# Loading each expert weight block by two 1 MB transfers, each half with its own semaphore

## The reference, cut to what matters

```python
def swiglu(h, w_gate, w_up, w_down):
    return (jax.nn.silu(h @ w_gate) * (h @ w_up)) @ w_down

def moe_swiglu(h, w_router, w_gate, w_up, w_down):
    t = h.reshape(B * S, D)
    logits = (t @ w_router).astype(jnp.float32)
    top_vals, top_idx = lax.top_k(logits, TOP_K)
    top_w = jax.nn.softmax(top_vals, axis=-1)
    gates = jnp.sum(jax.nn.one_hot(top_idx, N_EXPERTS, dtype=jnp.float32) * top_w[..., None], axis=1)
    out = jnp.zeros_like(t)
    for e in range(N_EXPERTS):
        out = out + swiglu(t, w_gate[e], w_up[e], w_down[e]) * gates[:, e:e + 1]
```

## Time and profile before

| | |
|---|---|
| median of three runs | 1361.24 us |
| lowest, highest | 1359.88, 1361.25 us |
| the profiled execution's own time | 1359.71 us |
| its span, first to last instruction | 1357.9 us |
| instructions in it | 16939 |
| PE busy in the span | 97% |
| DVE, ACT busy | 58%, 49% |
| bytes moved by DMA | 451.63 MB, mean 333 GB/s |

### The profile page before, as it was taken

How to read it: one execution, slowest core, us unless ns; L and a number is a source line. 1 busy time by engine, 2 the same in 40 slices (tenths; PEclk the granted TensorE clock), 3 DMA queues, 4 the chain that set the end, 5 groups by cost and what they waited for, 6 DMA issues and landing times.

```text
span 1357.9 us, 16939 instructions
## 1 busy us (share of the span) xinstructions
PE 1322.0 (97%) x6365; PEld 942.0 (69%) x6365; DVE 790.1 (58%) x912; ACT 661.4 (49%) x823; POOL 41.2 (3%) x45
## 2 busy tenths in 40 slices
PE   9999999999999999999999999999998899999996
PEld 8888788888888877865666656666555566665562
DVE  6556355555569667965466564665445566544463
ACT  5444445444454764854455454554444455444451
POOL 1000001000000012000000000000000000000000
PEclk9999999999999999999999999999999999999999
DMA  9745446555455518999999999999999999999995
GB/s 381 308 154 184 166 174 238 191 191 187 148 192 186 219 64 330 428 428 428 406 426 428 426 428 427 412 426 428 426 429 426 413 427 427 428 428 429 425 428 214
DMA packets 40448, 451.63 MB, mean 333 GB/s; under 512 B 4873, under 2 KB 5001, under 8 KB 8368
## 3 DMA queue, kind: packets, MB, share of 16 engines
q1 hardware_dynamic: 37408, 440.82, 79.8%
q0 software_dynamic: 2816, 9.63, 1.8%
q10 hardware_dynamic: 144, 0.09, 0.0%
HBM read 445.52 MB, written 6.55 MB: 333 GB/s over the span
## 4 chain that ended last, share of the span: by engine, by line
PE 80%; DMA 16%; DVE 2%; ACT 1%; issue 0%; POOL 0%; SPq 0%; DVEq 0%; ACTq 0%
PE psum L2013 19%; PE psum L2015 19%; PE psum L2014 19%; PE psum L2401 15%; DMA raw<-in_moe_w_gu 5%; DMA raw_more<-in_moe_w_gu 4%; DMA raw_first<-in_moe_w_gu 2%; DMA work<-in_moe_w_gu 2%; DMA raw<-in_moe_w_down 2%; PE psum L2059 1%; PE psum L2061 1%; PE psum L2060 1%; PE psum L2069 1%; DVE w_lo L1427 1%; PE psum L2439 1%; PE psum L2432 1%
## 5 line engine op out<-in xcount | busy, mean ns | idle before, releaser
L1427 DVE TENSOR_TENSOR w_lo<-raw,w_hi 128x1024 fp32r<-128x1024 f32 (+1 forms) x148 | 262.7, 1785 | 206.8 <-ACT w_hi L1060 206.2
L1060 ACT CAST w_hi<-raw 128x1024 fp32r<-128x1024 f32 (+1 forms) x148 | 221.4, 1504 | 218.2 <-PE psum L2015 152.9
L2015 PE MATMUL psum<-w_hi,actA_lo 128*128 128x512 f32 (+1 forms) x752 | 290.8, 387 | 0.0
L2013 PE MATMUL psum<-w_hi,actA_hi 128*128 128x512 f32 (+1 forms) x644 | 256.6, 398 | 18.8 <-DVE w_lo L1427 17.6
L2014 PE MATMUL psum<-w_lo,actA_hi 128*128 128x512 f32 (+1 forms) x644 | 248.3, 386 | 0.0
L2013 PEld LDWEIGHTS psum<-w_hi,actA_hi 128*128 128x128 f32 x644 | 121.4, 189 | 63.5 <-DVE w_lo L1427 25.0
L2015 PEld LDWEIGHTS psum<-w_hi,actA_lo 128*128 128x128 f32 x752 | 141.7, 188 | 29.9
L2401 PE MATMUL psum<-raw_more,const 128*64 128x512 f32 x608 | 137.4, 595 | 0.0
L2014 PEld LDWEIGHTS psum<-w_lo,actA_hi 128*128 128x128 f32 x644 | 121.7, 189 | 22.0
L1427 DVE TENSOR_TENSOR w_lo<-raw_more,w_hi 128x1024 fp32r<-128x1024 f32 x54 | 65.0, 1223 | 93.7 <-ACT w_hi L1060 93.3
L2013 PE MATMUL psum<-w_hi,actB_hi 128*128 128x512 f32 x292 | 114.8, 393 | 0.0
(11 more groups left out here) (280 smaller groups left out, 1940.0 us busy)
## 6 DMA issues: line engine op xcount, KB each, us to landing
raw_more<-in_moe_w_gu SPq DMA_DIRECT2D x45, 2048.0 KB, 26.5
raw<-in_moe_w_gu SPq DMA_DIRECT2D x37, 2048.0 KB, 25.0
raw<-in_moe_w_down SPq DMA_DIRECT2D x20, 2048.0 KB, 25.5
raw_more<-in_moe_w_down SPq DMA_DIRECT2D x20, 2048.0 KB, 26.5
work<-in_moe_w_gu SPq DMA_DIRECT2D x16, 2048.0 KB, 21.4
raw_first<-in_moe_w_gu SPq DMA_DIRECT2D x14, 2048.0 KB, 25.4
raw<-in_ret_w_in SPq DMA_DIRECT2D x22, 1024.0 KB, 10.3
raw_first<-in_moe_w_down SPq DMA_DIRECT2D x8, 2048.0 KB, 26.2
```

The source lines that it names most:

```text
L1060: nc.scalar.copy(hi_of(u)[:, 0:size], raw_of(w, u)[:, 0:size]).then_inc(sem["hi_ready"], 1)
L1427: nc.vector.tensor_tensor(lo_of(u)[:, 0:size], raw_of(w, u)[:, 0:size], as_f32(hi_of(u)[:, 0:size]), ALU.subtract).then_inc(sem["lo_ready" ...
L2013: nc.tensor.matmul(dst, l_hi[:, k, cols], r_hi[:, kk, rcols], start=first, stop=False)
L2015: return nc.tensor.matmul(dst, l_lo[:, k, cols], r_hi[:, kk, rcols], start=False, stop=last)
```

## The change

Every expert block of 2 MB is now loaded by two transfers, issued one behind the other: the first with columns 0 to 2047 of each partition (chunks 0 and 1, 8 KB of each partition's 16 KB), the second with columns 2048 to 4095. The first raises `two_in` of the slot, the second a new semaphore `rest_in` of the slot, nine new ones in all. ACT waits for `two_in` ahead of chunks 0 and 1 and for `rest_in` ahead of chunks 2 and 3. PE waits for `two_in` ahead of a short block and for `rest_in` between its second and third chunk. POOL's wait goes to `rest_in`. The two "down_half" transfers stay as they are. The waits for free slots stay as they are, and for the whole slot.

```diff
@@ def load(v, kind, expert, s, half, new):
                 if kind == "down_half":
                     src, dst = src[:, :, half * UNIT:(half + 1) * UNIT], dst[:, 0:UNIT]
-                sp.dma_start(dst, src.rearrange("o p n -> p (o n)")).then_inc(sem["two_in"][w.ring(v)], 16)
+                    sp.dma_start(dst, src.rearrange("o p n -> p (o n)")).then_inc(sem["two_in"][w.ring(v)], 16)
+                    return
+                sp.dma_start(dst[:, 0:UNIT], src[:, :, 0:UNIT].rearrange("o p n -> p (o n)")).then_inc(sem["two_in"][w.ring(v)], 16)
+                sp.dma_start(dst[:, UNIT:], src[:, :, UNIT:].rearrange("o p n -> p (o n)")).then_inc(sem["rest_in"][w.ring(v)], 16)
@@ POOL, ahead of the load of the experts' outputs
-            pool.wait_ge(sem["two_in"][w.ring(v)], w.block_in(v))
+            pool.wait_ge(sem["rest_in"][w.ring(v)], w.block_in(v))
@@ def hi_through(limit):
                         size, v = D, block_of(w, u)
-                        act.wait_ge(sem["two_in"][w.ring(v)], w.block_in(v))
+                        act.wait_ge(sem["two_in" if u % 4 < 2 else "rest_in"][w.ring(v)], w.block_in(v))
@@ PE
+            def rest_landed(v):
+                pe.wait_ge(sem["rest_in"][w.ring(v)], w.block_in(v))
@@ def short_hidden(at, s, v):
                     for kk in range(4):
+                        if kk == 2:
+                            rest_landed(v + half)
                         k = 4 * half + kk
@@ def short_down(at, s, v, loads=1):
                     for kk in range(4 // loads):
+                        if kk == 2:
+                            rest_landed(v)
                         k = 4 // loads * load + kk
```

More of the change, by code:

```diff
@@ L579, in stream @@
         for name in (["pe_done", "hi_ready", "lo_ready", "x_in0", "x_in1", "ident_in", "const_in", "small_in", "out_done"]
-                     + [f"raw_in{r}" for r in range(RAW_SLOTS)] + [f"two_in{r}" for r in range(FIRST_RAW)] + ["gain_in0", "gain_in1"]
+                     + [f"raw_in{r}" for r in range(RAW_SLOTS)] + [f"two_in{r}" for r in range(FIRST_RAW)] + [f"rest_in{r}" for r in range(FIRST_RAW)] + ["gain_in0", "gain_in1"]
                      + ["table_in", "zeroed", "sum_sq", "final_sq", "var", "rstd", "h_rows", "normed", "hn_scaled", "norm_hi", "norm_lo", "x_sum", "dve_step",
@@ L595, in stream @@
         sem["raw_in"] = [sem[f"raw_in{r}"] for r in range(RAW_SLOTS)]
-        sem["two_in"] = [sem[f"two_in{r}"] for r in range(FIRST_RAW)]
+        sem["two_in"], sem["rest_in"] = ([sem[f"{half}_in{r}"] for r in range(FIRST_RAW)] for half in ("two", "rest"))
         sem["gain_in"] = [sem["gain_in0"], sem["gain_in1"]]
```

## The result

The changed kernel takes 1372.26 us (median of 6 runs, 1370.53 to 1374.38) and the kernel before 1360.94 us in the same comparison (6 runs, 1359.42 to 1362.07). The medians lie 11.3 us apart. The ratio is put at 1.0087, a little above the quotient of the medians, with a 95% interval of 1.0077 to 1.0096, or 10.5 to 13.1 us. The forecast was 1373.0, from a sum of 11.8 us. The profiled execution of the changed kernel took 1374.38 us, the longest of the six, and its span is 1372.5 us.

The account below looks back on a forecast made before the run. The prediction took a saturated DMA stream (from 545 to 1320 us) plus a fixed tail to bound the kernel. 10.8 (rows) + 0.4 (run-up) + 0.6 (fetches) = 11.8 us, added to 1361.24, gave 1373.0 us, range 1362 to 1380 for 8 in 10.

Parts of the forecast that it names:

- Rows of a transfer: Saturated expert stream: 8 KB rows cost 0.07 us more per block, times 154 blocks, 10.8 us (ends 0 and 20).
- the two readings behind it: Cost per block from the trace: landing spacings gave 0.07 us, rates of 424 against 428 GB/s gave 0.046 us.
- Run-up: Before the saturated stretch: about six blocks pay the row cost too, 0.4 us, between 0 and 0.7.
- SP's issues: SP queue: one more 0.33 us issue per block, hidden by about five queued blocks, so nothing.
- Instructions fetched: Fetch queues: at most two more instructions per block, one or two more 16 KB packets, 0.6 us (0 to 1.2).
- Waits: PE, ACT and POOL: starting 2.5 us earlier on a block shortens one stall and lengthens the next, 0.
- PE's clock: Behind PE's stalls: lower-clock losses are made up from slack unless in the last 40 us; 0, at most 2.
- What would show it: Profile after: slices of 421 to 423 GB/s, DMA share 1, ACT and PE stalls about 12 us longer, tail 13.7 us.
- No change: Rival: other traffic explains 424 GB/s in the dense stretch, both row lengths run equally fast; 1361 us, chance 0.11.
- Half the price: Rival: stream blocks cost only 0.03 us more each, 5.2 us with fetches; 1366.5 us, chance 0.08.
- Faster: Rival: earlier hand-over shortens PE's stalls and frees slots sooner, at best 4 us gained; 1357 us, chance 0.07.
- Much slower: Rival: twice the outstanding transfers or split-row reads drop the rate, 5% being 38 us; 1400 us, chance 0.07.

Follow-up runs that it names:

- The experiment with one transfer: Kernel before with each block stored as two contiguous halves, loaded by one 2 MB transfer with 8 KB rows and one semaphore: 1373.51 us, ratio 1.0104.
- the down blocks: Changed kernel with only down blocks (52 of 154 in the saturated stretch) in two transfers, gu blocks loaded whole: 1365.43 us, ratio 1.0035.
- both halves waited for: Changed kernel with its transfers kept, but ACT and PE wait for both halves at the block's start: 1372.19 us, ratio 1.009.
- quarters: Kernel before with each block in four transfers of 512 KB, rows of 4 KB, a semaphore per chunk: 1400.07 us, ratio 1.0293.
- the last block whole and in quarters: Kernel before with its last down block in one transfer: 1360.72 us; with its very last 1 MB in two transfers of 512 KB: 1359.78 us.
- The even-and-odd kernel: Changed kernel with blocks cut by even and odd partitions, rows of 16 KB, both transfers waited for at the block's start: 1361.74 us, ratio 1.0008.
- the kernel with lower and upper partitions: Changed kernel with blocks cut into partitions 0 to 63 and 64 to 127, rows of 16 KB, both transfers waited for: 1879.22 us, ratio 1.3676.

## Why the prediction was right

**What bounds the kernel.** The reading held: a saturated stream with a fixed tail. The three experiments that shortened rows moved the end by the number of blocks times the change of one block and a little more: 13.5 us for 10.8, 4.8 for 3.6, 40 for 35. The one that changed only waits moved nothing.

**Rows of a transfer, 0.07 us per block, 10.8 us.** Right in kind and size. The experiment with one transfer shows the kind; the rates (4.970 - 4.900 = 0.070), the 10.2 us of the stream and the down blocks show the size. Of the two readings behind it, the spacing of landings (0.07) was the better one and the rate of the dense stretch (0.046) was too low, for a reason that the prediction itself named: 424 GB/s from 30 to 50 us include other traffic, at a share of 1.02. That other traffic may be what lifts it above 422. That the middle of the reading was right to within 0.004 us is luck: its own bounds were 0 and 0.13.

**Run-up, 0.4 us.** Not confirmed as a row cost; something larger stands there that the sum had no term for. The ten us at half clock put the profiled execution 3.7 us behind by SP's issue. The same block is issued late in the profiles of the other kernels with shorter rows as well: at 533.10 with one transfer, 529.88 with both halves waited for, 529.75 with quarters, for 528.00 before. It isn't theirs alone (the kernels with the last block whole and in quarters have 529.61 and 529.66), so a delay of 1.7 us comes without them too. The mean clocks of the six runs, as said above, leave one to three us of the 11.3 to PE's clock, and the sum of 11.8 has no term for them. It comes so near because 0.6 of fetches and 0.4 of run-up, neither of them shown, and 0.6 more for the stream than the profile has, stand in their place. That agreement is luck; the 10.8 of the stream isn't.

**SP's issues, nothing.** The sum was right, the reason not quite. SP's issues in the changed kernel from 985 us on (start, duration):

```profile
985.56 6.05 SPq L870 DMA_DIRECT2D raw<-in_moe_w_gu  x1
991.79 1.98 SPq L871 DMA_DIRECT2D raw<-in_moe_w_gu  x1
994.02 1.93 SPq L870 DMA_DIRECT2D raw_more<-in_moe_w_down  x1
```

The prediction took 0.33 us for each. Here they last 2 to 6 us, as if the queue took no more until something had left it; the trace doesn't show what SP waits for. It costs nothing: from 570 to 588 us an issue of the same kernel still lasts 0.33 us, and the rate of that stretch (422) is that of 1190 to 1240 us (421), where most last 2 to 6.

**Instructions fetched, 0.6 us.** The count was wrong. I had at most 334 more and said that no engine gets one from its waits; there are 485 more, so about 150 belong to the waits on PE and ACT. The fetch queues carry 4 packets more (q14 32 for 28, q8 unchanged), not one or two. The even-and-odd kernel has 756 more and costs 1.1 us with all its other extras, so 0.6 isn't ruled out, but an interval that starts at 0 doesn't show it, and its own price stays unmeasured.

**Waits, nothing.** Right in the stream, as the kernel with both waits shows. For the last block the prediction argued that it can't gain because it comes in halves already. True, but there is a second reason, the other branch of the tail: the adds of the experts' outputs end 0.7 us later than PE's branch would need, and so up to 0.7 us less work behind the last weights would not show.

**PE's clock, 0, at most 2; tail still 13.7.** This is where a small sum was missed. Behind the last landing the changed kernel took 14.4 us:

```profile
1353.06 1.94 PE L2404 MATMUL psum<-raw_first,const 128*64 128x512 f32 x8 [1.18 <-DMA raw_first<-in_moe_w_down]
1358.11 3.58 PE L2404 MATMUL psum<-raw,const 128*64 128x512 f32 x8 [3.11 <-DMA raw<-in_moe_w_down]
1362.48 1.99 PE L2550 MATMUL psum<-short_scaled,work 64*128 64x512 f32 x8 [0.79 <-ACT short_scaled L1406]
```

```profile
1357.88 4.63 DVE L1961 TENSOR_TENSOR x_sb<-x_sb,work 128x1024 f32<-128x1024 f32 x4 [5.13 <-DMA work<-y_dram]
1363.64 2.48 DVE L1818 TENSOR_TENSOR x_sb<-x_sb,psum 128x512 f32<-128x512 f32 x4 [1.13 <-PE psum L2550]
```

The same eight matmuls took 1.94 us for the half before and 3.58 for the last. In between PE stood idle for 3.11 us, and the granted clock from 1358 to 1362 was 0.57, near the lower level. The prediction had named this case ("unless it falls in the last 40 us") and took nothing for it in the sum. 1.6 us were lost on PE; at the end the tail is 0.7 longer, as DVE, busy until 1362.5, waited 1.13 us for PE, which it didn't before. The kernel that waits for both halves had no such stall (its last group took 1.94 us) and a tail of 13.5.

**What would show it.** 421 to 423 in the slices came as said, save where they dip as before. From 921 us on ACT's waits at the start of blocks in raw and raw_more are hardly longer in sum, though the kernel is slower. The third row is of its new wait:

```profile
ACT w_hi L1063 <- DMA raw<-in_moe_w_gu: 46.4, 6, 11.6
ACT w_hi L1063 <- DMA raw_more<-in_moe_w_gu: 34.4, 4, 9.8
ACT w_third L1063 <- DMA raw<-in_moe_w_gu: 3.6, 7, 0.7
```

46.4 us stand where 47.3 stood, and 34.4 where 34.1. But ACT now waits in a second place, ahead of the third chunk for `rest_in`, and all its waits for landings together are 129.6 us where they were 116.0. From 545 us on they are 141.8 for 124.4, and PE's wait for DVE is 21.0 for 17.6. So this sign came about as said, some 14 to 17 us for the 12; most of it stands in rows that the kernel before doesn't have.

**The rivals.** "No change" fell with the plateau of 421 and the ratio's interval. "Half the price" would need 425 GB/s; that is above every full slice after the seventeenth. "Faster" fell twice, since a byte costs more and the hand-over brings nothing even where rows and transfers are the same. "Much slower" fell with the rate, 1.4% down and not 5. The share of 1.01 didn't rule it out: the kernel with lower and upper partitions has the same share at half the rate. Nor did the 415 GB/s that the prediction set against it: part of POOL's 2 MB had moved before 1334.09 us, and the trace has 251 GB/s from there to 1344.17.

## What to carry to other kernels

When one stream of transfers is the only limit, time is the work of the DMA engines, and each row costs a fixed part beside its bytes: here 9 to 10 ns for rows of 4 to 16 KB, whatever the number of transfers. If a second semaphore is wanted, cut a transfer across the partitions, even and odd ones, and not along the row, and first ask whether an earlier hand-over moves anything: a stall that is shortened upstream of a saturated queue comes back at the next block. For such a change the quotient of two rates, taken where nothing else runs, times the number of blocks gives most of the forecast (here 10.8 of 11.3 us, and 35 of 40); what the start and the tail do with PE's clock it can't give.

## What the runs showed of the hardware that was not expected

- A transfer to partitions 0 to 63 followed by one to 64 to 127 halves the rate, 215 to 220 GB/s, at a DMA share of 1.00 to 1.01; even and odd partitions keep 428. In that kernel the rate rises late (362 GB/s from 1540 to 1600 us). Why wasn't looked into.
- SP's issue of a transfer isn't always 0.33 us. With rows of 8 KB it lasts 2 to 6 us once many are outstanding, also in the kernel with one transfer per block (1.5 to 4.4 us from 984 to 1003 us). With 16 KB rows in twice as many transfers it stays at 0.47 us in the same place. So it goes with the rows outstanding, and not with the transfers. The kernel with 4 KB rows fits: its transfers land 15.7 us after their issue where those of the changed kernel take 26.5, so at a time it has about three blocks of 512 rows outstanding, and the changed kernel five of 256.
- PE's clock was granted at half for 10 us in the choice of experts in the profiles of the changed kernel (0.50) and of the kernel with one transfer (0.56 from 515 to 525 us), at 0.66 and 0.67 from 520 to 525 us in those of the kernels with both halves waited for and with quarters, and at 1.00 in the one before and in the one with even and odd partitions. PE was busy all the time in the first case. What brought it, and whether it is the rows' doing, isn't settled.
